# The first projection tiles of a streaming hybrid layer, in pairs by seven block products

## What is computed

```python
h = layer_norm(x, ln_in_g, ln_in_b)          # 320 x 1024
u = h @ w_in                                 # 1024 x 14640, 115 tiles of 128 columns
u_gate, u_gla, u_rwkv, u_ssm = split(u)
us = u_rwkv + (previous_row(u_rwkv) - u_rwkv) * mu      # token shift, tiles 0 to 25
xbc = silu(causal_conv(u_xbc, w, bias))                 # tiles 27 to 50
```

## Time and profile before

| | us |
|---|---|
| median of 3 runs | 1502.66 |
| lowest and highest | 1501.89, 1505.04 |
| span of the profiled execution, first to last instruction | 1502.1 |
| TensorE busy in it | 1457.5 (97%) |
| VectorE, ScalarE, POOL busy | 647.1, 390.4, 116.8 |

### The profile page before, as it was taken

One profiled execution on the slowest core, in us unless ns is written; L12 is line 12 of the kernel. 1 busy time (PEld: TensorE's weight loads), 2 busy tenths in 40 slices (PEclk: granted clock), 3 DMA queues, 4 the chain that ended last, 5 costly groups with the idle time before them and its releaser, 6 DMA issues.

```text
span 1502.1 us, 31068 instructions
## 1 busy us (share of the span) xinstructions
PE 1457.5 (97%) x13071; PEld 1011.2 (67%) x13071; DVE 647.1 (43%) x1227; ACT 390.4 (26%) x874; POOL 116.8 (8%) x107
## 2 busy tenths in 40 slices
PE   7999999999999999999999999999999999999995
PEld 6776667677776777767766765766666767675751
DVE  5223778875644677734541114622211112121228
ACT  2112444442322554435431011111111111111111
POOL 3000113121010000000000000000000001000000
PEclk9999999999999999999999999999999999999998
DMA  7778375563344544565577538689999999999985
GB/s 243 168 174 181 101 214 166 132 203 97 103 130 147 138 112 116 178 180 163 135 231 263 157 100 359 251 337 399 417 423 430 428 426 429 426 428 429 427 342 211
DMA packets 157017, 375.27 MB, mean 250 GB/s; under 512 B 101708, under 2 KB 110300, under 8 KB 139216
## 3 DMA queue, kind: packets, MB, share of 16 engines
q1 hardware_dynamic: 123712, 341.35, 63.9%
q10 hardware_dynamic: 26592, 15.49, 3.5%
q0 software_dynamic: 6576, 16.48, 3.2%
HBM read 327.14 MB, written 51.95 MB: 252 GB/s over the span
## 4 chain that ended last, share of the span: by engine, by line
PE 82%; DVE 7%; DMA 4%; ACT 2%; DVEq 2%; issue 1%; SPq 1%; ACTq 1%; POOLq 0%
PE PS L576 27%; PE PS L1069 14%; PE PS L919 8%; PE PS L1036 7%; PE PS L1088 6%; PE PS L624 4%; PE PS L1041 2%; PE PS L957 2%; DVE region L1492 2%; DVE region L1499 2%; PE PS L632 1%; ACT L1172 1%; PE PS L1052 1%; PE PS L1077 1%; PE PS L817 1%
## 5 line engine op out<-in xcount | busy, mean ns | idle before, releaser
L576 PE MATMUL PS<-h0T,region 128*128 128x320 f32 x1808 | 510.2, 437 | 1.0 <-issue 0.8
L576 PEld LDWEIGHTS PS<-h0T,region 128*128 128x128 f32 x1808 | 336.8, 190 | 144.6 <-issue 12.2
L1172 ACT ACTIVATE region<-PS 128x9 f32<-128x9 f32 (+6 forms) x407 | 148.5, 383 | 681.9 <-PE PS L576 311.8
L1069 PE MATMUL PS<-region 128*64 128x512 f32 x1024 | 228.8, 592 | 0.0
L1069 PEld LDWEIGHTS PS<-region 128*64 128x64 f32 x1024 | 124.5, 137 | 92.2 <-issue 31.9
L1492 DVE TENSOR_TENSOR region<-region 128x256 f32<-128x256 f32 (+10 forms) x210 | 127.0, 624 | 96.8 <-ACTq L1218 76.2
L919 PE MATMUL PS<-region 128*128 128x320 f32 x512 | 138.6, 433 | 1.3 <-DMA region<-wo 1.2
L919 PEld LDWEIGHTS PS<-region 128*128 128x128 f32 x512 | 97.0, 190 | 42.5 <-issue 1.7
L1172 ACT ACT_TABLE_LOAD x80 | 102.6, 1283 | 73.1 <-DMA region<-projected 56.7
L1088 PE MATMUL PS<-region,history 128*64 128x512 f32 x512 | 119.7, 596 | 1.0 <-ACTq L1454 0.7
L1172 ACT ACTIVATE region<-region 128x256 f32<-128x256 f32 (+8 forms) x160 | 81.2, 531 | 147.9 <-DMA region<-projected 37.0
(11 more groups left out here) (210 smaller groups left out, 1163.8 us busy)
## 6 DMA issues: line engine op xcount, KB each, us to landing
region<-moe_w SPq DMA_DIRECT2D x64, 2048.0 KB, 17.4
region<-moe_w SPq DMA_DIRECT2D x64, 1024.0 KB, 15.0
region<-w_in SPq DMA_DIRECT2D x115, 512.0 KB, 5.6
region<-wo SPq DMA_DIRECT2D x32, 512.0 KB, 3.6
projected<-region ACTq DMA_DIRECT2D x65, 167.5 KB, 3.9
expert_rows<-region SPq DMA_DIRECT2D x20, 512.0 KB, 7.2
region<-expert_rows SPq DMA_DIRECT2D x5, 2048.0 KB, 14.4
region<-projected SPq DMA_DIRECT2D x10, 768.0 KB, 6.3
```

The costliest lines, as they stand in the source:

```text
L576: last = mm(PS[:, 6 + i % 2, 0:NTOK], WR[:, i, k, :], H0T[:, k, :], start=(k == 0), stop=(k == KT - 1))
L1069: last = mm(PS[tiles(i), 2, :], XE[:, k, tiles(i)], W13[r][i][:, k * 512:k * 512 + 512], start=(k == 0), stop=(k == KT - 1))
L1172: return nc.scalar.activation(out, in_, f, **kw)
```

## The change

Tiles 4 to 27 are taken in 12 pairs (a, b). Each pair is a product of a 2 x 2 block matrix of weights (tile a or b by first or second half of the 1024 inputs, each four k-steps of 128) with a 2 x 2 block matrix of inputs (half of the inputs by half of the tokens: the first or the last 32 of each chunk). The eight block products are replaced by seven, each of four k-steps by 160 columns, so 28 code matmuls of 160 columns instead of 16 of 320. In return there are sums: four of the token blocks, once (`TSUM`, 128x640 each); four of the weight blocks for each pair (`WSUM`, 128x512 each, VectorE); and four adds of 160 columns to the results for each pair (VectorE). The products gather in three banks (X, Z, W), other ones for even and odd pairs; ScalarE copies four of the seven intermediate states of them to `STG` (`keep`), VectorE adds the rest (`quads`), ScalarE writes the history columns from `STG` (`edges`), VectorE shifts the two tiles. The stores of a pair are issued one pair later, behind the `keep`s of the next and ahead of its `edges`. Both weight tiles of a pair are freed in the fifth product. VectorE's order is: token sums, shifts 0 to 3, weight sums of pairs 0 and 1, then for each pair its quads, its shifts and the weight sums of the pair after the next. `tile_moved` counts by two at the end of a pair. Besides, `LNB` moves to an address that `USS` doesn't touch, so SP's wait for `h_kept` goes, POOL drains behind each of its six instructions instead of behind three, and five semaphores share names with others (`x_first`, `x_rest` and `x_last` with `halves_in`, `shared_in` and `router_in`).

```diff
+        TSUM = shaped(OT[:, 8:16].rearrange("p a b -> p (a b)"), 4, KT // 2, NTOK // 2)
+        spare = OT[:, 16:].rearrange("p a b -> p (a b)")[:, 2 * D:]
+        WSUM = [shaped(v, 4, KT // 2, 128) for v in (spare[:, 0:2048], tail)]
+        H0H = H0T.rearrange("p k (c h w) -> p k h c w", c=NCH, h=2)
+        KH = KT // 2
+        def quad_sum(b):
+            return shaped(PS[:, b, 0:NTOK // 2], NCH, L // 2)
+        def quad_out(i, j):
+            return STG[:, i, :, HIST + 32 * j:HIST + 32 * j + 32]
...
-        LNB = shaped(REGION[:, mixer_base:mixer_base + 2 * D], 2, D)
+        LNB = shaped(REGION[:, lnb_base:lnb_base + 2 * D], 2, D)
...
             with sp.Fori(1, 4) as m:
                 for i in range(RING):
                     weights(m, i)
-            sp.wait_ge(sem("h_kept"), 1)
             first_rows(0, 10)
...
+            def project_pair(m, u):
+                pair, a, b = m * 2 + u - 2, 2 * u, 2 * u + 1
+                X, Z, W = (quad_sum(3 * u + x) for x in range(3))
+                def product(out, lhs, rhs, start, freed=False):
+                    for k in range(KH):
+                        last = mm(out, lhs(k), rhs(k), start=start and k == 0, stop=k == KH - 1, skip_group_check=True)
+                        if freed and k < 2:
+                            last.then_inc(sem("tile_done"), 1)
+                    last.then_inc(sem("quad"), 1)
+                for i in (a, b):
+                    pe.wait_ge(sem(f"weights_in{i}"), (m + 1) * 16)
+                pe.wait_ge(sem("quads_out"), pair + 1)
+                product(X, lambda k: WR[:, a, k, :], lambda k: H0H[:, k, 0], True)
+                product(Z, lambda k: WR[:, b, KH + k, :], lambda k: TSUM[:, 3, k], True)
+                pe.wait_ge(sem("weights_summed"), pair + 1)
+                pe.wait_ge(sem("quad_kept"), pair * 4 + 1)
+                product(X, lambda k: WSUM[u][:, 1, k], lambda k: TSUM[:, 1, k], False)
+                pe.wait_ge(sem("quad_kept"), pair * 4 + 2)
+                product(Z, lambda k: WR[:, a, KH + k, :], lambda k: H0H[:, KH + k, 0], True)
+                product(W, lambda k: WSUM[u][:, 0, k], lambda k: TSUM[:, 0, k], True, True)
+                pe.wait_ge(sem("quad_kept"), pair * 4 + 3)
+                product(X, lambda k: WSUM[u][:, 2, k], lambda k: TSUM[:, 2, k], False)
+                pe.wait_ge(sem("quad_kept"), pair * 4 + 4)
+                product(W, lambda k: WSUM[u][:, 3, k], lambda k: H0H[:, KH + k, 1], False)
...
+            pe.wait_ge(sem("token_sums"), 1)
             with pe.Fori(1, PRE // RING) as m:
-                for i in range(RING):
-                    project(m, i)
+                for u in range(2):
+                    project_pair(m, u)
             pe.drain().then_inc(sem("phase_over"), 1)
...
-            for n in range(PRE):
+            def keep(p, made, i, j, region):
+                act.wait_ge(sem("quad"), 7 * p + made)
+                a_(quad_out(i, j), region, ACT.Copy)
+                act.drain().then_inc(sem("quad_kept"), 1)
+            def edges(n):
+                i = n % RING
+                act.wait_ge(sem(f"store_done{i}"), (n // RING + 1) * 16)
+                src = STG[:, i, :, HIST:CW]
+                a_(STG[:, i, 1:NPC, 0:HIST], src[:, 0:NPC - 1, L - HIST:L], ACT.Copy)
+                a_(STG[:, i, 0:NCH:NPC, 0:HIST], HISTS[:, n, :, :], ACT.Copy)
+                if n >= T_XBC:
+                    k = n - T_XBC
+                    a_(CVO[:, :, k, :], src[:, NPC - 1:NCH, L - HIST:L], ACT.Copy)
+                    a_(CV[:, i], src, ACT.Identity, scale=VEC[:, V_CW + 72 + k:V_CW + 73 + k], bias=VEC[:, V_CB + k:V_CB + k + 1])
+                elif n < T_MISC:
+                    a_(SHO[:, :, n], src[:, NPC - 1:NCH, L - 1], ACT.Copy)
+            def tile_out(n):
+                i = n % RING
+                if n < T_MISC:
+                    act.wait_ge(sem("tile_mixed"), n + 1)
+                    act.dma_start(ut[n, :, :, HIST:CW], CV[:, i]).then_inc(sem(f"store_done{i}"), 16)
+                elif n < T_XBC:
+                    act.wait_ge(sem("tile_moved"), n + 3)
+                    act.dma_start(ut[n, :, :, :], STG[:, i, :, :]).then_inc(sem(f"store_done{i}"), 16)
+            for n in range(RING):
                 move(n // RING, n % RING)
+            for p in range(PAIRS):
+                u, a, b = p % 2, 2 * (p % 2), 2 * (p % 2) + 1
+                act.wait_ge(sem("tile_mixed"), 2 * p + 2)
+                X, Z, W = (quad_sum(3 * u + x) for x in range(3))
+                keep(p, 1, a, 0, X)
+                keep(p, 2, b, 0, Z)
+                keep(p, 3, a, 1, X)
+                keep(p, 5, b, 1, W)
+                if p > 0:
+                    for n in (RING + 2 * p - 2, RING + 2 * p - 1):
+                        tile_out(n)
+                act.wait_ge(sem("quads_out"), p + 3)
+                for n in (RING + 2 * p, RING + 2 * p + 1):
+                    edges(n)
+                act.drain().then_inc(sem("tile_moved"), 2)
+            for n in range(PRE - 2, PRE):
+                tile_out(n)
...
+            dve.wait_ge(sem("h0T_ready"), EVICTED)
+            for out, x, y in ((0, H0H[:, 0:KH, 1], H0H[:, 0:KH, 0]), (2, H0H[:, KH:, 1], H0H[:, 0:KH, 1]),
+                              (1, H0H[:, KH:, 1], TSUM[:, 0]), (3, H0H[:, KH:, 0], TSUM[:, 1])):
+                tt(TSUM[:, out].rearrange("p k (c w) -> p k c w", c=NCH), x, y if out in (0, 2) else
+                   y.rearrange("p k (c w) -> p k c w", c=NCH), sub)
+                dve.drain()
+            nc.vector.sem_inc(sem("token_sums"), 1)
+            nc.vector.sem_inc(sem("quads_out"), 2)
             dve.wait_ge(sem("vectors_in"), 32)
...
-            for n in range(T_MISC):
+            def quads(p):
+                u, a, b = p % 2, 2 * (p % 2), 2 * (p % 2) + 1
+                X, Z, W = (quad_sum(3 * u + x) for x in range(3))
+                dve.wait_ge(sem("quad"), 7 * p + 4)
+                dve.wait_ge(sem("quad_kept"), 4 * p + 1)
+                tt(quad_out(a, 0), quad_out(a, 0), Z, add)
+                dve.wait_ge(sem("quad"), 7 * p + 6)
+                dve.wait_ge(sem("quad_kept"), 4 * p + 4)
+                for j in range(2):
+                    tt(quad_out(b, j), quad_out(b, j), X, add)
+                dve.wait_ge(sem("quad"), 7 * p + 7)
+                tt(quad_out(a, 1), quad_out(a, 1), W, add)
+                dve.drain().then_inc(sem("quads_out"), 1)
+            flat2 = lambda x: x.rearrange("p a b -> p (a b)")
+            def weight_sums(p):
+                u, a, b = p % 2, 2 * (p % 2), 2 * (p % 2) + 1
+                S1, S2, S3, S4 = (flat2(WSUM[u][:, x]) for x in range(4))
+                A11, A12, A21, A22 = (flat2(WR[:, i, k * KH:k * KH + KH, :]) for i in (a, b) for k in range(2))
+                for i in (a, b):
+                    dve.wait_ge(sem(f"weights_in{i}"), (p // 2 + 2) * 16)
+                if p > 1:
+                    dve.wait_ge(sem("quad"), 7 * p - 7)
+                tt(S1, A21, A22, add)
+                tt(S3, A11, A21, sub)
+                dve.drain()
+                tt(S2, S1, A11, sub)
+                dve.drain()
+                tt(S4, A12, S2, sub)
+                dve.drain().then_inc(sem("weights_summed"), 1)
+            for n in range(RING):
                 shift(n)
+            for p in range(2):
+                weight_sums(p)
+            for p in range(PAIRS):
+                quads(p)
+                for n in range(RING + 2 * p, min(RING + 2 * p + 2, T_MISC)):
+                    shift(n)
+                if p + 2 < PAIRS:
+                    weight_sums(p + 2)
...
+            def keep_rows(t, k):
+                w = 128 if t < 2 else 64
+                ptt(H0[0:w, t, :], H0[0:w, t, :], LNB[0:w, k, :], add if k else mul)
+                pool.drain()
             pool.wait_ge(sem("h0T_ready"), EVICTED)
             pool.wait_ge(sem("ln_in"), 32)
-            for k, op in ((0, mul), (1, add)):
+            for k in range(2):
                 for t in range(TT3):
-                    w = 128 if t < 2 else 64
-                    ptt(H0[0:w, t, :], H0[0:w, t, :], LNB[0:w, k, :], op)
-                pool.drain()
-            nc.gpsimd.sem_inc(sem("h_kept"), 1)
+                    keep_rows(t, k)
```

30 lines of the change are left out of this document (17 added, 13 removed).

## The result

The kernel after takes **1526.3 us** (median of 4 runs, 1525.66 to 1529.86), the kernel before 1503.85 us beside it (4 runs, 1501.89 to 1507.33): a ratio of 1.0157, 95% interval 1.0137 to 1.0177. The forecast was 1508.4 us with a range of 1500 to 1518. The direction was right, the size was not: 22 us were lost, not 6, and no rival but the loads in series (1540) lay that high, whose mechanism did not happen. The profiled execution took 1525.76 us, its span is 1524.0 us.

What follows compares the result with a forecast made beforehand. TensorE, busy 97% of the span, was taken as the bound; pairs -7.8, start +9.3 and end +4.2 us made +5.7, giving 1508.4 us on the median of 1502.66, range 1500 to 1518.

Steps and rivals of the forecast that it cites:

- loads in series: Rival: TensorE's weight loads set record spacing, 192 ns each, 10.75 us a pair; total 1540 us; chance 0.03.
- The stream: TensorE's block products: 56 records of 160 columns at 139 ns, 7.78 us a pair instead of 8.61.
- the spacing of 195 ns: TensorE record spacing estimated by the Trainium skill's ratio for load and matmul together; the forecast took 139 ns instead.
- VectorE and ScalarE: Steady pairs: VectorE has 6.6 us of work, ScalarE under 4; a loop of 7.5 us fits in 7.78.
- The weight queue: Steady pairs: second weight load takes 7.2 us, making pairs 7.9 us; 7.8 us gained over 11 pairs.
- The end: Stage end: tile 28 waits 1.9 us for edges, last rows wait for late stores; cost 4.2 us.
- queue-bound pairs: Rival: weight loads over 7.2 us, landing after 8.6, lengthen each pair to 8.6; total 1516 us; chance 0.14.
- the prediction's signs of being wrong: TensorE without idle from 25 to 50 us, pairs of 7.5 us, or L645 under 10 us after the last product.
- The start: Token sums wait out GpSimd's LayerNorm instructions, TensorE idles until 36.2 us, pair 0 ends at 52.0; cost 9.3 us.
- the 0.8 us for it: Tile 3: extra time added to its 4.31 us for matmuls starting after an idle TensorE.
- The prediction's upper bound of 3.9 us: Tile 3: most extra time if TensorE falls to 1.2 GHz after idling, double time.
- The clock: Idle TensorE falls to 1.2 GHz; applied only to tile 3's upper bound, with later phases the same work shifted.

Runs made afterwards that it cites:

- Run 1: Kernel after, with SyncE loading first rows 0-7, 8-15 and 16-25 instead of 0-9, 10-17 and 18-25 at the same queue places: 1519.32 us.
- run 3: Kernel after, with ScalarE issuing the stores of the pair before ahead of the copy behind which they stood: 1519.95 us, ratio 1.0104 to the kernel before.
- run 4: Kernel after, with GpSimd's six LayerNorm instructions waiting until pair 1 has been added up: 1530.18 us, ratio 1.0172 to the kernel before.
- run 9: Kernel after, GpSimd's LayerNorm rows moved to the merge phase, weight sums ahead of shift 3, first rows in four pieces, last pair's stores earlier: 1507.93 us.
- run 5: Kernel after, with unread matmuls in two TensorE idle times, 11 ahead of tile 3 and 7 ahead of L690: 1525.57 us, ratio 1.0142 to before.
- run 12: Kernel after, unchanged, run again for a second profile: 1531.68 us.

## Why the prediction was wrong

**The stream was right.** 139 ns a record were forecast (134.5 to 145), 135.8 measured; the pair without waits is 7.61 us, inside 7.53 to 8.12. Loads in series is out, and with it the spacing of 195 ns by the Trainium skill's ratio.

**VectorE and ScalarE** kept up in the steady state. The weight sums of a pair take 2.84 us against 2.95; VectorE is busy 5.9 us a pair where 6.6 were added up.

**The weight queue** is the step that failed. It was priced as a tax on each pair (7.9 us instead of 7.78, by a second load of 7.2 us), and the load alone was looked at. In a steady pair the second load lands after 4.5 to 6.0 us and sets nothing. What was left out is that SyncE's queue holds two loads of the first rows *between* those of the weights, and that these wait for the very stores that the change puts last. The prediction followed this wait only behind the stage ("The end"), for the third piece. The price was 13.3 us in the stage. Runs 1 and 3 take away the wait, and 10.7 and 7.8 us go with it in the eleven pairs. In place of 7.8 us gained, the eleven pairs lost 2.3. The rival of queue-bound pairs, a second load of over 7.2 us, came true in the two stalled pairs (8.2 and 9.75 us beside the rows) and in one behind them (8.3), but run 3 shows that loads of 7.0 to 8.35 us cost at most 1.1 us at a time. None of the prediction's signs of being wrong would have shown this step.

**The start** was forecast at 9.3 us and cost 10.4. The mechanism held: token sums two to four behind GpSimd, TensorE idle to 36.21 (36.2 forecast). The token-sum row shows it, VectorE from 19 to 33 us:

```profile
19.96 3.72 DVE L1584 TENSOR_TENSOR region<-h0T 128x640 f32<-128x640 f32 x2 [0.24 <-ACTq L1238]
23.76 5.69 DVE L1584 TENSOR_TENSOR region<-h0T,region 128x640 f32<-128x640 f32 x2
29.74 2.26 DVE L1584 TENSOR_TENSOR region<-region 128x320 f32<-128x320 f32 x1 [0.29 <-issue]
```

and runs 4 and 9, without GpSimd there, the other side of it (1.73 us for two). Tile 3 ended at 42.24 instead of 41.3: the clock was at 1.2 GHz to 39.5, so the 0.8 us for it were 1.7. The rule cited from the Trainium skill (TensorE: Matmul & The Clock Gate, Part 1) agrees in kind: 0.71 is the granted clock of the window of tile 3. The prediction's upper bound of 3.9 us (double time for 4.31 us would be 4.3) was not reached, since 3.5 us of the stretch fell in the idle time.

**The clock** elsewhere was a term of zero in the sum, though the prediction had this rule for tile 3. By half their length the five stretches behind the start cost some 8.5 us: 3.4 inside the 13.3 above, the rest in the later phases, whose work is that of before and was put at nothing. This is the second step that failed, by an estimate: only tile 3, the records at 97.60 and runs 5 and 12 price a stretch directly.

**The end** was forecast at 4.2 us and cost 4.9: tile 28 waits 1.73 us (1.9 forecast), the LoRA product comes 14.7 us after the last product (13.9 forecast). The last two stores, which leave together, need 7.8 and 8.1 us, not 6.0, and the rows only 5.3, not 6.4.

**By the sum:** forecast -7.8 + 9.3 + 4.2 = +5.7. Measured -11.0 + 13.3 + 10.4 + 4.9 = +17.6 at the LoRA product, and 4.3 behind it. Run 1 shows what is left of the error without the two stalls: -8.4 in the pairs, +10.0 at the start, +6.2 at the end, +7.8 at the LoRA product (155.0 against 147.2), near the forecast's +5.7; and 6.5 behind it, where nothing was forecast, with three stretches of 3.4 us and the end of one of 6.8 there (6.9 by half their length). Its total, 15 us over the kernel before, is so still well above the forecast. What stays open is why a stretch comes where it comes: the kernel before waits 1.1 us where the kernel after waits 1.20 (978 us) and keeps 2.4 GHz, and run 5, made to take stretches away, was no faster and had others.
